# Two-layer hybrid decoder on one core: activation rows at one byte offset modulo 256, high-weight slots at four

## The reference

```python
def swiglu(x, w_gate, w_up, w_down):
    return (jax.nn.silu(x @ w_gate) * (x @ w_up)) @ w_down
...
    for i in range(DEPTH):
        g = norm_gains[i]
        j = i // 2
        y = swiglu(rms_norm(h, g[0]), ffn_w_gate[i, 0], ffn_w_up[i, 0], ffn_w_down[i, 0])
        h = h + 0.5 * rms_norm(y, g[1])
        u = rms_norm(h, g[2])
        if i % 2 == 0:
            y = mixer_ab(u, ab_w_in[j], ab_conv_w[j], ab_a_log[j], ab_dt_bias[j], ab_out_norm[j], ab_w_out[j])
        else:
            y = mixer_cd(u, cd_w_in[j], cd_sinks[j], cd_w_out[j])
        h = h + rms_norm(y, g[3])
        y = swiglu(rms_norm(h, g[4]), ffn_w_gate[i, 1], ffn_w_up[i, 1], ffn_w_down[i, 1])
        h = h + 0.5 * rms_norm(y, g[5])
    return h[:, N_META:]
```

## The kernel before

| operand | high | low |
|---|---|---|
| weights, every slot | 128 | 128 |
| `u`, k = 0 | 128 | 0 |
| `u`, k = 1 ("ab") | 0 | 128 |
| `u`, k = 2 | 64 | 192 |
| `u`, k = 3 | 192 | 64 |
| `u`, k = 4 ("cd") | 128 | 0 |
| `u`, k = 5 (256 tokens) | 64 | 192 |
| `hid`, first to third block | 0, 64, 128 | 128, 192, 0 |
| `hid`, last block | 192 | 64 |

## Time and profile before

### The profile page before, as it was taken

How to read it: one execution, slowest core, us unless ns; L and a number is a source line. 1 busy time by engine, 2 the same in 40 slices (tenths; PEclk the granted TensorE clock), 3 DMA queues, 4 the chain that set the end, 5 groups by cost and what they waited for, 6 DMA issues and landing times.

```text
span 1098.2 us, 19370 instructions
## 1 busy us (share of the span) xinstructions
PE 1086.0 (99%) x8599; PEld 1054.9 (96%) x8599; DVE 703.8 (64%) x770; ACT 544.6 (50%) x635; POOL 1.6 (0%) x13
## 2 busy tenths in 40 slices
PE   9999999999999999999999999999999999999997
PEld 8999999999999999999999999999999899999986
DVE  6755644488996777655546765654578867666552
ACT  5644343467555765342545643443465766444441
POOL 0000000000000000000000000000000000000000
PEclk9999999999999999999999999999999999999999
DMA  9656555958751445554553755555553244656451
GB/s 315 191 184 185 183 172 156 161 106 198 147 169 40 154 153 159 188 179 153 177 183 118 229 160 186 170 161 171 190 177 116 78 154 154 190 184 203 153 173 39
DMA packets 173072, 180.02 MB, mean 164 GB/s; under 512 B 7508, under 2 KB 165804, under 8 KB 172988
## 3 DMA queue, kind: packets, MB, share of 16 engines
q1 hardware_dynamic: 172668, 177.66, 53.8%
q10 hardware_dynamic: 320, 1.11, 0.3%
HBM read 177.05 MB, written 1.71 MB: 163 GB/s over the span
## 4 chain that ended last, share of the span: by engine, by line
PE 93%; DVE 3%; ACT 2%; issue 1%; DMA 1%; ACTq 0%; DVEq 0%
PE ps L1799 24%; PE ps L1801 24%; PE ps L1800 24%; PE ps L1904 6%; PE ps L1888 2%; PE ps L1889 2%; PE ps L1887 2%; PE ps L2029 2%; PE ps L1871 1%; PE ps L1833 1%; PE ps L1836 1%; PE ps L1837 1%; DVE hT L1227 1%; DVE yT L1226 1%; DMA x_tok<-meta_tokens 1%
## 5 line engine op out<-in xcount | busy, mean ns | idle before, releaser
L1799 PE MATMUL ps<-u,w_hi 128*128 128x272 f32 (+1 forms) x1648 | 473.3, 287 | 0.7 <-DVE w_lo L1178 0.4
L1801 PE MATMUL ps<-u,w_lo 128*128 128x272 f32 (+1 forms) x1648 | 471.3, 286 | 0.0
L1800 PE MATMUL ps<-u,w_hi 128*128 128x272 f32 (+1 forms) x1648 | 469.8, 285 | 0.0
L1178 DVE TENSOR_TENSOR w_lo<-raw,w_hi 128x2048 fp32r<-128x2048 f32 (+2 forms) x167 | 369.4, 2236 | 108.0 <-ACT w_hi L716 107.9
L716 ACT ACTIVATE w_hi<-raw 128x2048 fp32r<-128x2048 f32 (+2 forms) x167 | 310.4, 1869 | 166.1 <-PE ps L1801 143.6
L1799 PEld LDWEIGHTS ps<-u,w_hi 128*128 128x128 f32 x1648 | 309.8, 188 | 2.8 <-issue 1.0
L1800 PEld LDWEIGHTS ps<-u,w_hi 128*128 128x128 f32 x1648 | 310.1, 188 | 0.3
L1801 PEld LDWEIGHTS ps<-u,w_lo 128*128 128x128 f32 x1648 | 309.6, 188 | 0.0
L1801 PE MATMUL ps<-hid,w_lo 128*128 128x272 f32 x528 | 152.4, 289 | 0.0
L1799 PE MATMUL ps<-hid,w_hi 128*128 128x272 f32 x528 | 152.1, 288 | 0.0
L1800 PE MATMUL ps<-hid,w_hi 128*128 128x272 f32 x528 | 151.6, 287 | 0.0
(11 more groups left out here) (345 smaller groups left out, 1045.5 us busy)
## 6 DMA issues: line engine op xcount, KB each, us to landing
raw<-ffn_w_up SPq DMA_DIRECT2D x44, 1024.0 KB, 5.4
raw<-ffn_w_gate SPq DMA_DIRECT2D x43, 1024.0 KB, 5.4
raw<-ffn_w_down SPq DMA_DIRECT2D x24, 896.0 KB, 4.8
raw<-ffn_w_down SPq DMA_DIRECT2D x20, 1024.0 KB, 5.1
raw<-ab_w_in SPq DMA_DIRECT2D x16, 1024.0 KB, 14.3
raw<-cd_w_in SPq DMA_DIRECT2D x9, 1024.0 KB, 5.9
raw<-ab_w_out SPq DMA_DIRECT2D x4, 1024.0 KB, 7.0
raw<-cd_w_out SPq DMA_DIRECT2D x4, 1024.0 KB, 5.3
```

The source lines that it names most:

```text
L1178: dve.tensor_tensor(dst, src, w_hi[:, n % NW, 0:rows(n) * CB].bitcast(F32), ALU.subtract)\
L1799: pe.matmul(o, wh, rhs_hi[:, kk, tok], start=first and kk == 0, stop=False)
L1800: pe.matmul(o, wh, rhs_lo[:, kk, tok], start=False, stop=False)
L1801: ins = pe.matmul(o, wl, rhs_hi[:, kk, tok], start=False, stop=last and kk == rows(n) - 1)
```

## The change

It changes where operands lie, and nothing else: on each engine the same instructions stand in the same order with the same shapes and waits.

- A row of `u` or `hid` takes 1280 bytes (`ROW` = 320), and all low rows stand behind all high rows. Since 1280 is 5 x 256, high and low rows have the same offset modulo 256.
- That offset is 64 for every sublayer but the last, and 128 for the last.
- A slot of `w_hi` takes 8256 bytes (`SLOT`), 64 more than before. Slots 0 to 3 start at 128, 192, 0 and 64 modulo 256. `raw` and `w_lo` stay at 128.
- Small tables (the norm gains, the small "ab" weights, head masks and the like) move into the 32 columns that a row of `u` leaves free, and `h_tok` moves to the place of the squares. Other arrays slide accordingly.

Modulo 256 the table becomes:

| operand | high | low |
|---|---|---|
| weights, slots 0, 1, 2, 3 | 128, 192, 0, 64 | 128 |
| `u`, k = 0 to 4 | 64 | 64 |
| `u`, k = 5 | 128 | 128 |
| `hid`, first three blocks | 64 | 64 |
| `hid`, last block | 128 | 128 |

```diff
+SLOT = RAW + 16
...
-ROW = 576
-LOW = 288
-U_AT = (0, 128, 192, 64, 0, 192)
-HID_AT = (0, 64, 128, 192)
+ROW = 320
+SPARE = 288
+PLACE = 64
+U_AT = (0, 0, 0, 0, 0, 64)
+HID_AT = (0, 0, 0, 64)
...
-        w_hi = sb("w_hi", [NW, RAW], F32R)
+        w_hi = sb("w_hi", [NW, SLOT], F32R)
+        ss = sb("ss", [T])
+        rstd = sb("rstd", [2, T])
+        u_place = place[0]
+        assert u_place % 256 == PLACE
+        u_room = sb("u_room", [2, KD, ROW], F32R)
+
+        def parts(name, rows_, where, shift):
+
+            both = at(name, [P, 2 * rows_ * ROW], F32R, where)[:, :].rearrange("p (z k c) -> p z k c", z=2, c=ROW)
+            cols = slice(shift // 4, shift // 4 + T)
+            return both[:, 0, :, cols], both[:, 1, :, cols]
+
+        inputs = [parts(f"u_{k}", KD, u_place, shift) for k, shift in enumerate(U_AT)]
+        spare = at("spare", [P, 2 * KD, ROW], F32, u_place)[:, :, SPARE:ROW]
...
-        def high_low(name, rows_, where):
-
-            both = at(name, [P, rows_ * ROW], F32R, where)[:, :].rearrange("p (k c) -> p k c", c=ROW)
-            return both[:, :, 0:T], both[:, :, LOW:LOW + T]
...
-        hid_place = arena + (-arena) % 256
-        hid_end = hid_place + KF * ROW * 4 + max(HID_AT)
-        hidden = {where: high_low(f"hid_{where}", KF, hid_place + where) for where in dict.fromkeys(HID_AT)}
+        hid_place = arena + (PLACE - arena) % 256
+        hid_end = hid_place + 2 * KF * ROW * 4
+        hidden = [parts(f"hid_{f}", KF, hid_place, shift) for f, shift in enumerate(HID_AT)]
...
-                u_hi, u_lo = inputs[U_AT[k]]
-                hid_hi, hid_lo = hidden[HID_AT[f % 4]]
+                u_hi, u_lo = inputs[k]
+                hid_hi, hid_lo = hidden[min(f, 3)]
```

More of the change, by code:

```diff
@@ L175, in build @@
         w_lo = at("w_lo", [P, NR, RAW], F32R, ring)
-        w_hi = sb("w_hi", [NW, RAW], F32R)
+        w_hi = sb("w_hi", [NW, SLOT], F32R)
[10 more added lines that the diff above has]
+        spare = at("spare", [P, 2 * KD, ROW], F32, u_place)[:, :, SPARE:ROW]
         hT = sb("hT", [KD, T])
         yT = sb("yT", [KD, T])
-        u_place = place[0]
-        sb("u_room", [KD * ROW + max(U_AT) // 4], F32R)
-        def high_low(name, rows_, where):
-            both = at(name, [P, rows_ * ROW], F32R, where)[:, :].rearrange("p (k c) -> p k c", c=ROW)
-            return both[:, :, 0:T], both[:, :, LOW:LOW + T]
-        inputs = {where: high_low(f"u_{where}", KD, u_place + where) for where in dict.fromkeys(U_AT)}
-        ss = sb("ss", [T])
         lnv = sb("lnv", [T])
-        rstd = sb("rstd", [2, T])
         ident = sb("ident", [P])
         ones = sb("ones", [P])
-        gains = sb("gains", [12 * KD])
+        w_ba, gains = spare[:, 0:KD, :], spare[:, KD:KD + 3, :]
+        small = [spare[:, KD + 3 + n // 2, n % 2 * 16:n % 2 * 16 + 3 * HG] for n in range(8)]
+        singles = spare[:, 2 * KD - 1, :]
+        group_sum, head_of, dt4, alog4, out_norm = (singles[:, c0:c0 + n] for c0, n in
+                                                    ((0, 2 * HG), (8, HG), (12, HG), (16, HG), (20, 1)))
         masks = sb("masks", [N_MASKS, P])
         center = sb("center", [P])
-        head_of = sb("head_of", [HG])
         convw = sb("convw", [4 * 12])
[L198 to L202, removed]
         scratch = place[0]
@@ L534, in gain @@
             g = (layer * 6 + s) * KD + m
-            return gains[:, g:g + 1]
+            return gains[:, g // 32, g % 32:g % 32 + 1]
         def norm_of(k):
@@ L917, in ab @@
                 act.wait_ge(s_x, 1)
[L918 to L921, removed]
+                step.done(act.activation(small[2][:, :], small[1][:, :], ACT.Exp, scale=-1.0))
+                step.done(act.activation(small[2][:, :], small[2][:, :], ACT.Ln, bias=1.0))
+                act.activation(small[3][:, 0:HG], alog4[:, :], ACT.Exp)
+                act.activation(small[4][:, :].rearrange("p (t h) -> p t h", h=HG), ba[:, :, 0:HG], ACT.Exp, scale=-1.0)\
                     .then_inc(s_xe, 1)
@@ L1273, in ab @@
             def ab(k, b):
-                sm = [small[:, n, :].rearrange("p (t h) -> p t h", h=HG) for n in range(8)]
+                sm = [small[n][:, :].rearrange("p (t h) -> p t h", h=HG) for n in range(8)]
                 to = {"gq": gq, "gk": gk, "gv": gv, "rk": rk, "rq": rq, "rv": rv, "rg": rg, "gz": gz}
@@ L1729, in _ @@
             dve.wait_ge(s_gT, 1)
-            dve.tensor_copy(gains[:, :], ps[:, 0, 0:12 * KD]).then_inc(s_gains, 1)
+            dve.tensor_copy(gains, ps[:, 0, 0:12 * KD].rearrange("p (r c) -> p r c", c=32)).then_inc(s_gains, 1)
             for g in range(2):
@@ L1768, in _ @@
                         w = w_ba[:, :, 0:2 * HG]
-                        dve.tensor_tensor(w, w, over(gains[:, g0:g0 + KD], [P, KD, 2 * HG]), ALU.mult)\
+                        dve.tensor_tensor(w, w, over(gains[:, g0 // 32, g0 % 32:g0 % 32 + KD], [P, KD, 2 * HG]), ALU.mult)\
                             .then_inc(s_wba, 1)
```

27 lines of the change are left out of this document (13 added, 14 removed).

## The result

The changed kernel took **1105.32 us** (median of five runs, 1104.96 to 1106.56), against 1100.0 us before: 1.0046 times as long, with a 95% interval of 1.0033 to 1.0060. It is slower by 0.46%, where 1094.0 us was forecast. The profiled execution has a span of 1104.7 us, 6.5 more than before.

What follows compares the result with a forecast made beforehand. PE was taken as the bound, through the distance between matmul starts. From 1099.96 us, 7.6 gained with 272 columns and 1.7 lost with 256 gave 1094 us; own range 1091 to 1098, 8 in 10 from 1084 to 1103.

Steps and rivals of the forecast that it cites:

- What bounds the kernel: Whole kernel: PE busy 1086.0 of 1098.2 us at full clock, so time is matmul count times distance between starts.
- Activations at 64: 272-column matmuls: 123.8 ns for all of them, together 7.6 us gained.
- 128/128 with 256 columns: Last sublayer's `u` matmuls, activations at 128: 118.3 ns, the middle of 116.7 and 120.0, 1.7 us lost.
- the last projection: Last down projection, 512 columns, weights stream and `hid` is loaded: no change taken, bounds 1.2 us either way.
- Small tables: Tables with a stride of 1280 bytes, on other engines: nothing taken; 2 us if some 40 instructions each cost 50 ns.
- I take the lower one because rows 6 and 7 are the nearest: 272-column chunks in the other `w_hi` slots: 123.8 ns chosen from bounds 123.8 and 126.9, since activations match.
- Its reading of single offsets: Short `first_tiles` blocks, 272 columns, weights at 128: offset 64 costs 123.8 ns, 192 and 0 126.3 to 126.9.
- Distance to the weights decides: Rival, chance 0.13: weight-minus-activation offset sets the pace, mean 124.9 ns by slot with 272 columns, 1102.3 us, slower.
- its worse form: Rival, chance 0.10: all 272-column matmuls at 126.6 ns as in the first down projection, 1112 us.
- Staggered slots free more: Rival, chance 0.12: high weights at other offsets collide less, pace 121.2 ns, 15 us more saved, 1079 us.
- chunks whose pace changes with n % 4: Sign in the 272-column stretches that the forecast is wrong and weight-to-activation distance sets the pace; no size given.

Runs made afterwards that it cites:

- the rows alone: The changed kernel with all slots of `w_hi` back at offset 128 and everything else in its place: 1093.47 us, ratio 0.9933.
- the second sweep: The changed kernel with high weights all at 0, low weights still at 128, and other offsets of `u` and `hid` per sublayer: 1103.21 us.

## Why the prediction was wrong

**What bounds the kernel**: right. No sum but that of starts explains the difference, and VectorE and ScalarE don't matter for it.

**Activations at 64**: right, as the rows alone show. Forecast were 123.8 ns and −7.6 us with +1.7 for 256 columns, −5.9 in all; measured 123.33 and −6.4. By parts: 128/128 with 256 columns was taken at 118.3 and came at 117.77; the last projection was taken as unchanged and was (233.33). The 118.3 was luck: the blocks of the earlier trace rows that the prediction gives as 64 and 192 are read from 128 and 0, 64 bytes further on, and the new place is read from 192, for which it had no row.

**Small tables**: nothing taken, nothing measured in the gaps between sublayers, and the rows alone have them too.

**The step that failed** is the slots: "I take the lower one because rows 6 and 7 are the nearest". That sentence takes 123.8 ns for all slots. The bound that was not taken, 126.9, was nearly what came: 126.13 over the gate, up and down stretches of 272 columns. Against the rows alone, the three feed-forward blocks lose 2.8 ns on 4389 matmuls, 12.2 us. A part is the paces that the offsets settle in when all slots are alike: their mean of 124.25 is 0.92 over 123.33, 4.0 us. The larger part, 1.9 ns or 8.2 us, has no row before the change and no place in the sum: the pattern that one chunk leaves to the next. The prediction took a pace for a property of addresses. Its reading of single offsets from the blocks of rows 6 to 9 rests on that too; the 123.8 for 64 came true in the rows alone, but with the slots at 64 the same blocks and the long stretch behind them differ by some 4 ns.

Between the two profiled spans (1091.8 and 1104.7) lie 12.9 us. By the starts of the matmuls, 12.2 are those of the blocks, 2.6 lie between the first block and the third sublayer's stretch (1.6 of them the wait in "ab", 1.9 us against 0.3), 0.7 in the later norms and "cd"; 1.2 us are won back in the last sublayer, and 1.4 at the start, where the profiled execution of the rows alone began its stretch later. Why the round trip lands later in "ab" wasn't tried.

**The rivals.** "Distance to the weights decides" had the sign and the neighbourhood (1102.3), and its paces by slot, 123.8, 125.7, 125.7 and 124.4, come near to what the offsets give alone (123.33, 125.9, 125.55, 122.23); its worse form (126.6 for all) comes near to the pace that was measured. Neither has the reason: by distance, slots 0 and 3 should be the fast ones, and in the changed kernel they are the slowest. "Staggered slots free more" was wrong of the stagger, though a pace under 123.8 exists, with all slots at 64. In the Trainium skill ("TensorE: Matmul & The Clock Gate", "Step-by-step: what each phase is for") the rule is that a weight load takes no read bandwidth from the running matmul. What the prediction drew from it, that the slots' offsets would do nothing, did not come true: moving the high weights alone, from 128 to 0 or 64, turned 123.33 into 125.55 or 122.23 ns. Whether the two compete for reads, no run here shows.

**What would show it wrong** was well chosen: "chunks whose pace changes with n % 4" is what the timeline has. But it was set down as the sign of the distance rival, and distance isn't the reason.

What stays open is the mechanism: which accesses meet, and why a pattern holds itself. That it holds, over how many matmuls, and which chunks set it off is shown; a model of the reads that gives these numbers is not.

## What to carry to other kernels

Where a long run of matmuls is bound by its own pace, the byte offsets modulo 256 of weights and activations can be worth some per cent (here 1105.3 us against 1082.6 with the same work), and are to be tried on the chip as whole layouts, first with all slots of a ring at the same offset: a price that was measured for one operand in one place doesn't add up with another. A single chunk that lies elsewhere can slow everything behind it (or speed it up) until the stream is broken, so a ring whose slots lie at different offsets is suspect. And whoever moves a ring's slots between two stages should look at which old slot the new one touches, and at what is queued behind that wait: here it hid 10 us of gain.

## What the runs showed that was not expected

- The same instructions on the same addresses have two settled paces: 123.33 or 126.67 ns with 272 columns (weights at 128, rows at 64), 117.77 or 113.33 with 256 columns (weights at 128, rows at 128 and read from 192). Which one holds is decided by what ran before, and lasted over all that followed: 1200 matmuls and more with 272 columns, over 800 with 256.
- An offset can be the best or among the worst: 64 gives 122.23 where all slots have it and the stretch begins behind another matmul, some 126.5 behind `first_tiles`, and 126.7 behind a chunk at any other offset.
- The number of columns matters beyond their count: high weights at 0 and activations read from 192/192 give 113.33 for 256 columns, 0.443 ns a column, and 124.5 for 272 (`hid` in the first down projection of the second sweep, which follows another stretch), 0.458.
